# The high half of a weight against both halves of the tokens in one 512-column matmul

## The chip, the core and the metric

The program runs on one core of a Trainium2 chip. Its time is that of the device in microseconds for one launch; lower is better. A run of the kernel before is taken beside every run of another kernel on the same chip.

The engines of the core work side by side and meet only at semaphores. TensorE (PE in the rows) multiplies matrices, with a weight load (PEld) ahead of each matmul. VectorE (DVE), ScalarE (ACT) and GpSimd (POOL) do elementwise work, and SyncE (SP) starts most DMAs.

## The reference

Two blocks are computed on 256 tokens of width 1024, in float32. The first has two layers; each layer has a feed-forward stage, a mixer of four branches (two convolutions, two attentions), and a second feed-forward stage. The second block has an attention and a recurrent branch with a context of 256 more tokens and then a mixture of 32 experts. Only the four feed-forward stages of the first block matter here:

```python
D_MODEL = 1024; SEQ = 256; DEPTH = 2; D_FF = 2816

def _swiglu(x, w_gate, w_up, w_down):
    return (jax.nn.silu(x @ w_gate) * (x @ w_up)) @ w_down

for l in range(DEPTH):
    x = x + 0.5 * _swiglu(_rmsnorm(x, ffn1_norm[l]), ffn1_w_gate[l], ffn1_w_up[l], ffn1_w_down[l])
    ...
    x = x + 0.5 * _swiglu(_rmsnorm(x, ffn2_norm[l]), ffn2_w_gate[l], ffn2_w_up[l], ffn2_w_down[l])
```

## The kernel before

The program is a row of phases with a barrier between them. Activations are kept with features on the 128 partitions and the 256 tokens along the free dimension.

**Products in two halves.** TensorE multiplies here in the type fp32r, in which a number keeps fewer bits than float32. Each float32 operand is therefore split: `hi` is the number in fp32r, `lo` is what is left. A product is the sum of three: w_hi x_hi, w_hi x_lo and w_lo x_hi. The function `product` (L242) issues them as three matmuls of 256 columns, all accumulating in the same half bank of PSUM.

**A feed-forward stage** (`ffn_program`, L423) first normalizes x; VectorE and ScalarE write the halves `h_hi` and `h_lo` of the result, eight slices `k` of 128 features. Then it goes over 22 chunks `c` of 128 hidden features. For a chunk there are three weight tiles of 128 x 1024: `g` (gate), `u` (up) and `d` (down), each with two buffers `a`. The work on them is this:

- SyncE loads the tiles into `raw` (L442), three DMAs a chunk; a load waits until VectorE has made the `lo` half (`g_lo`, `u_lo`, `d_lo`) of the tile that was in the buffer.
- ScalarE casts each to `hi` (`upper`, L492), then computes silu of the gate part from PSUM into `sil` (L501).
- VectorE subtracts to make `lo` (`lower`, L515); then it multiplies `sil` by the up part in PSUM into `hid` (L523), and splits `hid` into two halves by a cast (L250) and a subtraction (L252).
- TensorE computes `gate_up(c)`: 2 x 8 products, 48 matmuls, into the PSUM bank 4 + a, the gate part in one half of it and the up part in the other. `down(c)` are 8 products, 24 matmuls, of the down tile with the halves of `hid`; they accumulate over all chunks in banks 0 to 3.

The order on each engine is as it is written. TensorE goes gate_up(c + 1), down(c), so that the hidden part of chunk c is made while gate_up(c + 1) runs. VectorE's turn for chunk c is: `lower` of gate and up of chunk c + 1, `lower` of down of chunk c, then wait for silu, `hid`, cast, subtraction. ScalarE's turn is: cast of gate and up of chunk c + 1, cast of down of chunk c, then silu of chunk c, for which it waits for TensorE alone (and for `hid` of two chunks before).

**GpSimd in these stages.** Beside this, in each of the four stages, GpSimd computes a quarter of a matrix-vector product that the second block needs (`ada_pool`, L377). It loads twelve tiles of `w_ada` with its own DMAs (L398), multiplies them by a row (L403, 16 such products, 128 x 1024) and adds each up by halving (L390: widths 512, 256, 128). It is done with that before the stage is.

Of the kernel before, what the change touches and what calls it, by code (L numbers as in the profile page):

```python
# [14 lines left out]
F32R = mybir.dt.float32r  # L15
I32 = mybir.dt.int32
ALU = mybir.AluOpType
ACT = mybir.ActivationFunctionType
# [344 lines left out]
def ffn_phase(nc, B, I, l, which, wg, wu, wd, gain):  # L363

    with ExitStack() as ctx:
        (raw, sil, hid) = alloc(nc, ctx, B, raw=(P, 6, D), sil=(P, 2, T), hid=(P, 2, T))
        (hi, lo, hid_hi, hid_lo) = alloc(nc, ctx, B, F32R, hi=(P, 6, D), lo=(P, 6, D), hid_hi=(P, 2, T), hid_lo=(P, 2, T))
        (B.c_rows, B.wada, B.adaprod, B.adasum) = alloc(
            nc, ctx, B, c_rows=(P, 2, D), wada=(P, 2, D), adaprod=(P, D), adasum=(P, 2 * ADA_CTX + ADA_X, D // 8))
        ffn_program(nc, B, l, dict(g=wg, u=wu, d=wd), gain, raw, hi, lo, sil, hid, hid_hi, hid_lo, (I["w_ada"], which))  # L370
# [52 lines left out]
def ffn_program(nc, B, l, src, gain, raw, hi, lo, sil, hid, hid_hi, hid_lo, ada):  # L423
    x, ps, con = B.x, B.ps, B.con
    acc = ps[:, 0:4, :].rearrange("p b (c t) -> p (b c) t", t=T)
    gu = [ps[:, 4 + a, :].rearrange("p (w t) -> p w t", t=T) for a in range(2)]
# [3 lines left out]
    with phase(nc, NORM + ADA + names + " gu_done silu_done hid_mul hid_hi_done hidden_ready down_done x_done") as (block, s):  # L430
# [16 lines left out]
        def _(pe):  # L447
# [5 lines left out]
            def gate_up(c, a):  # L453
                wait(pe, s["hidden_ready"], c - 1)
                for j, kind in enumerate("gu"):
                    pe.wait_ge(s[f"{kind}_lo"], c + 1)
                    for k in range(KD):
                        if kind == "g" and isinstance(c, int) and c == 0:
                            pe.wait_ge(s["h_lo_done"], k + 1)
                        w = slice(k * P, (k + 1) * P)  # L460
                        mm = product(nc, gu[a][:, j, :], hi[:, slot[kind] + a, w], lo[:, slot[kind] + a, w],
                                     B.h_hi[:, k, :], B.h_lo[:, k, :], k == 0, k == KD - 1)
# [22 lines left out]
        def _(act):  # L485
# [8 lines left out]
            def turn(c, a, end, i):  # L494
# [4 lines left out]
                act.wait_ge(s["gu_done"], c + 1)  # L499
                wait(act, s["hid_mul"], c - 1)  # L500
                nc.scalar.activation(sil[:, a, :], gu[a][:, 0, :], ACT.Silu).then_inc(s["silu_done"], 1)  # L501
# [9 lines left out]
        def _(dve):  # L511
# [5 lines left out]
            def turn(c, a, end, i):  # L517
# [3 lines left out]
                lower("d", c, a)  # L521
                dve.wait_ge(s["silu_done"], c + 1)
                nc.vector.tensor_tensor(hid[:, a, :], sil[:, a, :], gu[a][:, 1, :], ALU.mult).then_inc(s["hid_mul"], 1)  # L523
# [469 lines left out]
def first_block_program(nc, B, I):  # L993

    B.stage = "first"
    with ExitStack() as ctx:
        (B.vec, B.nsink, B.swa_table) = alloc(nc, ctx, B, vec=(P, NVEC), nsink=(P, 4), swa_table=(P, 4 * TC, T))
        B.h_hi, B.h_lo = alloc(nc, ctx, B, F32R, h_hi=(P, KD, T), h_lo=(P, KD, T))
# [1064 lines left out]
```

## Time and profile before

| | |
|---|---|
| runs | 3191.58, 3196.12, 3221.68 us; median 3196.12 |
| span of the profiled execution | 3212.8 us |
| its own time | not shown apart; it is at least the span |
| mean granted TensorE clock | 0.915 of full speed |
| TensorE busy, matmuls | 2749.1 us (86%), 17040 |
| VectorE busy | 1658.3 us (52%), 2343 instructions |
| ScalarE busy | 788.1 us (25%), 1190 instructions |
| GpSimd busy | 608.7 us (19%), 410 instructions |
| `lower` of the feed-forward stages (L515) | 264, 497.1 us busy, 1926 ns each |
| feed-forward stages, first to last silu | 63 to 243, 597 to 777, 830 to 1011, 1365 to 1544 us |

The stages can be told by the silu on L501, of which there are 22 in each. A matmul is pipelined: the time shown for one (some 0.28 us) is longer than the distance to the next, so TensorE's pace is read from the starts. A time that VectorE or GpSimd shows for one instruction runs from its start to its end and includes what it waited for in between.

### The profile page before, as it was taken

To read this page: it belongs to the slowest core of one execution; us is meant where nothing else is said; L and a number is where in the kernel's file an instruction comes from. 1 tells how busy PE (TensorE), PEld (TensorE's weight loads), DVE (VectorE), ACT (ScalarE), POOL (GpSimd) and SP (SyncE) were. 2 spreads that over 40 slices of the span, in tenths; PEclk is the share of its full clock that TensorE was granted. 3 is DMA by queue.
4 is the path that set the end of the run, shared out by engine and by line. 5 is a ranking of instruction groups with operands and counts; after the bars stand their busy time and mean duration, and the time that the engine had idled before them with its cause. 6 is when DMAs were issued, how large, how long until landed. Compare 5 with 4: busy or idle time off the path is not lost. (4 is left out here: it accounts for less than half of the span.)

```text
span 3212.8 us, 44631 instructions
## 1 busy us (share of the span) xinstructions
PE 2749.1 (86%) x17040; PEld 2031.2 (63%) x17040; DVE 1658.3 (52%) x2343; ACT 788.1 (25%) x1190; POOL 608.7 (19%) x410
## 2 busy tenths in 40 slices
PE   5998888898898898699598697568998999989986
PEld 4998777798798896699488565533433333333333
DVE  4974665994984376697413665342223233232323
ACT  2334441433343442234223321100000000000000
POOL 2940000770960000293000000001001101011010
PEclk9999879899899898899798798779789999999998
DMA  5653431563563351365114110539899999999993
GB/s 215 231 177 131 151 111 53 205 233 139 182 223 118 119 169 53 138 229 208 42 65 158 39 53 1 211 134 355 346 390 378 410 410 410 410 410 410 410 407 155
DMA packets 186745, 697.77 MB, mean 217 GB/s; under 512 B 20611, under 2 KB 22019, under 8 KB 185091
## 3 DMA queue, kind: packets, MB, share of 16 engines
q1 hardware_dynamic: 178742, 662.00, 54.6%
q0 software_dynamic: 7488, 29.36, 2.4%
q10 hardware_dynamic: 432, 5.33, 0.4%
q8 instruction: 48, 0.79, 0.1%
q14 instruction: 35, 0.29, 0.0%
HBM read 694.54 MB, written 2.11 MB: 217 GB/s over the span
## 5 line engine op out<-in xcount | busy, mean ns | idle before, releaser
L515 DVE TENSOR_TENSOR lo_first<-raw_first,hi_first 128x1024 fp32r<-128x1024 f32 x264 | 497.1, 1926 | 42.6 <-ACT hi_first L492 40.7
L1704 PE MATMUL ps<-wexp_all_second,hg_second 128*64 128x512 f32 x2112 | 475.5, 597 | 41.5 <-DMA wexp_all_second<-in_w_lin 24.3
L243 PE MATMUL ps<-h_hi_first,hi_first 128*128 128x256 f32 x1408 | 409.1, 291 | 48.9 <-DVE h_lo_first L234 48.8
L244 PE MATMUL ps<-h_lo_first,hi_first 128*128 128x256 f32 x1408 | 404.6, 287 | 0.0
L245 PE MATMUL ps<-h_hi_first,lo_first 128*128 128x256 f32 x1408 | 404.4, 287 | 0.0
L1704 PEld LDWEIGHTS ps<-wexp_all_second,hg_second 128*64 128x64 f32 x2112 | 149.4, 137 | 358.1 <-issue 283.9
L492 ACT CAST hi_first<-raw_first 128x1024 fp32r<-128x1024 f32 x264 | 267.8, 1048 | 206.0 <-DMA raw_first<-in_ffn_wg 132.0
L243 PEld LDWEIGHTS ps<-h_hi_first,hi_first 128*128 128x128 f32 x1408 | 275.7, 196 | 56.2 <-DVE h_lo_first L234 30.7
L243 PE MATMUL ps<-h_hi_first,w_hi_first 128*128 128x256 f32 x960 | 275.9, 287 | 34.7 <-DVE w_lo_first L338 23.8
L1792 DVE TENSOR_TENSOR sq_whole<-ps,con_all_whole 64x512 f32<-64x512 f32 x132 | 90.8, 688 | 402.8 <-POOL con_all_whole L1684 349.2
L244 PEld LDWEIGHTS ps<-h_lo_first,hi_first 128*128 128x128 f32 x1408 | 276.9, 197 | 0.0
L245 PEld LDWEIGHTS ps<-h_hi_first,lo_first 128*128 128x128 f32 x1408 | 276.7, 197 | 0.0
L244 PE MATMUL ps<-h_lo_first,w_hi_first 128*128 128x256 f32 x960 | 273.6, 285 | 0.0
L245 PE MATMUL ps<-h_hi_first,w_lo_first 128*128 128x256 f32 x960 | 273.3, 285 | 0.0
L1704 PE MATMUL ps<-wexp_all_second,aT_second 128*64 128x512 f32 x1056 | 244.0, 616 | 23.5 <-ACT aT_second L1771 23.5
L1792 DVE TENSOR_TENSOR y_second<-ps,con_all_whole 64x512 f32<-64x512 f32 x66 | 45.4, 688 | 324.7 <-PE ps L1704 324.2
L390 POOL TENSOR_TENSOR adaprod_first<-adaprod_first 128x512 f32<-128x512 f32 (+1 forms) x128 | 209.2, 1634 | 10.0
L243 PEld LDWEIGHTS ps<-h_hi_first,w_hi_first 128*128 128x128 f32 x960 | 186.3, 194 | 38.3 <-DVE w_lo_first L338 20.7
L338 DVE TENSOR_TENSOR w_lo_first<-raw_first,w_hi_first 128x1024 fp32r<-128x1024 f32 x120 | 146.8, 1225 | 117.5 <-ACT w_hi_first L313 106.6
L243 PE MATMUL ps<-hid_hi_first,hi_first 128*128 128x256 f32 x704 | 200.2, 284 | 4.8 <-DVE hid_lo_first L252 4.6
L244 PE MATMUL ps<-hid_lo_first,hi_first 128*128 128x256 f32 x704 | 199.2, 283 | 0.0
L245 PE MATMUL ps<-hid_hi_first,lo_first 128*128 128x256 f32 x704 | 199.2, 283 | 0.0
(354 smaller groups left out, 4635.8 us busy)
## 6 DMA issues: line engine op xcount, KB each, us to landing
wexp_all_second<-in_w_gate SPq DMA_DIRECT2D x66, 2048.0 KB, 17.7
wexp_all_second<-in_w_lin SPq DMA_DIRECT2D x66, 2048.0 KB, 24.6
wexp_all_second<-in_w_down SPq DMA_DIRECT2D x66, 2048.0 KB, 23.0
raw_first<-in_ffn_wg SPq DMA_DIRECT2D x88, 512.0 KB, 5.4
raw_first<-in_ffn_wu SPq DMA_DIRECT2D x88, 512.0 KB, 6.7
raw_first<-in_ffn_wd SPq DMA_DIRECT2D x88, 512.0 KB, 3.3
raw_first<-in_w_g SPq DMA_DIRECT2D x64, 512.0 KB, 3.3
wada_first<-in_w_ada POOLq DMA_DIRECT2D x48, 512.0 KB, 7.1
```

The costliest lines, as they stand in the source:

```text
L243: nc.tensor.matmul(out, w_hi, x_hi, start=start, stop=False, skip_group_check=True)
L244: nc.tensor.matmul(out, w_hi, x_lo, start=False, stop=False, skip_group_check=True)
L245: return nc.tensor.matmul(out, w_lo, x_hi, start=False, stop=stop, skip_group_check=True)
L338: nc.vector.tensor_tensor(B.w_lo[:, slot], B.raw[:, slot], B.w_hi[:, slot].bitcast(F32), ALU.subtract).then_inc(s[f"{tag}_lo"], 1)
L390: add = lambda out, x, width: nc.gpsimd.tensor_tensor(out, x[..., 0:width], x[..., width:2 * width], ALU.add)
L492: nc.scalar.copy(hi[:, slot[kind] + a % 2], raw[:, slot[kind] + a % 2]).then_inc(s[f"{kind}_hi"], 1)
L515: nc.vector.tensor_tensor(lo[:, j], raw[:, j], hi[:, j].bitcast(F32), ALU.subtract).then_inc(s[f"{kind}_lo"], 1)
L1704: mm = nc.tensor.matmul(dst[side(half), :], lhs(k), B.wexp[2 * "gld".index(kind) + part][:, k % 4, half * HALF:(half + 1) * HALF], start=( ...
L1792: last = tt(dst[side(half), :], bank[side(half), :], B.bias[side(half), n * D + half * HALF:n * D + (half + 1) * HALF], ALU.add)
```

## The change

`h_hi` and `h_lo` now lie side by side in one tile `h_pair`, 512 columns for each slice k. In `gate_up` the high half of a weight meets both in one matmul of 512 columns, which fills a whole PSUM bank: w_hi x_hi in columns 0 to 255, w_hi x_lo in columns 256 to 511. The third product, w_lo x_hi, is added to the first 256 columns. Gate and up so take a bank each, and a buffer `a` two banks (4 and 5, or 6 and 7; the mean square of the norm, in bank 6, is read before chunk 1 writes there). VectorE adds the two parts of gate and of up in one tensor_reduce that reads 1024 elements of PSUM in each partition and writes 512 to `sil` in SBUF. ScalarE takes silu of the gate part there, in place, once the reduce is done; VectorE's product `hid` then reads both operands from SBUF. `down` is as it was.

```diff
--- before.py
+++ after.py
@@ -363,7 +363,7 @@
 def ffn_phase(nc, B, I, l, which, wg, wu, wd, gain):
 
     with ExitStack() as ctx:
-        (raw, sil, hid) = alloc(nc, ctx, B, raw=(P, 6, D), sil=(P, 2, T), hid=(P, 2, T))
+        (raw, sil, hid) = alloc(nc, ctx, B, raw=(P, 6, D), sil=(P, 2, 2, T), hid=(P, 2, T))
         (hi, lo, hid_hi, hid_lo) = alloc(nc, ctx, B, F32R, hi=(P, 6, D), lo=(P, 6, D), hid_hi=(P, 2, T), hid_lo=(P, 2, T))
         (B.c_rows, B.wada, B.adaprod, B.adasum) = alloc(
             nc, ctx, B, c_rows=(P, 2, D), wada=(P, 2, D), adaprod=(P, D), adasum=(P, 2 * ADA_CTX + ADA_X, D // 8))
@@ -423,11 +423,11 @@
 def ffn_program(nc, B, l, src, gain, raw, hi, lo, sil, hid, hid_hi, hid_lo, ada):
     x, ps, con = B.x, B.ps, B.con
     acc = ps[:, 0:4, :].rearrange("p b (c t) -> p (b c) t", t=T)
-    gu = [ps[:, 4 + a, :].rearrange("p (w t) -> p w t", t=T) for a in range(2)]
+    gu = [ps[:, 4 + 2 * a:6 + 2 * a, :] for a in range(2)]
     ms = ps[:, 6, 0:T]
     slot = {"g": 0, "u": 2, "d": 4}
     names = " ".join(f"w{k}{a}" for k in "gud" for a in range(2)) + " " + " ".join(f"{k}_{h}" for k in "gud" for h in ("hi", "lo"))
-    with phase(nc, NORM + ADA + names + " gu_done silu_done hid_mul hid_hi_done hidden_ready down_done x_done") as (block, s):
+    with phase(nc, NORM + ADA + names + " gu_done added silu_done hid_mul hid_hi_done hidden_ready down_done x_done") as (block, s):
         s.update(std=B.std[:, 0:T], var=B.var[:, 0:T], rstd=B.rstd[:, 0:T])
 
         @block.gpsimd
@@ -458,8 +458,10 @@
                         if kind == "g" and isinstance(c, int) and c == 0:
                             pe.wait_ge(s["h_lo_done"], k + 1)
                         w = slice(k * P, (k + 1) * P)
-                        mm = product(nc, gu[a][:, j, :], hi[:, slot[kind] + a, w], lo[:, slot[kind] + a, w],
-                                     B.h_hi[:, k, :], B.h_lo[:, k, :], k == 0, k == KD - 1)
+                        nc.tensor.matmul(gu[a][:, j, :], hi[:, slot[kind] + a, w], B.h_pair[:, k, :], start=(k == 0),
+                                         stop=False, skip_group_check=True)
+                        mm = nc.tensor.matmul(gu[a][:, j, 0:T], lo[:, slot[kind] + a, w], B.h_hi[:, k, :], start=False,
+                                              stop=(k == KD - 1), skip_group_check=True)
                 mm.then_inc(s["gu_done"], 1)
 
             def down(c, a):
@@ -496,9 +498,8 @@
                     upper("g", c + 1, a + 1, i)
                     upper("u", c + 1, a + 1, i)
                 upper("d", c, a, i)
-                act.wait_ge(s["gu_done"], c + 1)
-                wait(act, s["hid_mul"], c - 1)
-                nc.scalar.activation(sil[:, a, :], gu[a][:, 0, :], ACT.Silu).then_inc(s["silu_done"], 1)
+                act.wait_ge(s["added"], c + 1)
+                nc.scalar.activation(sil[:, a, 0, :], sil[:, a, 0, :], ACT.Silu).then_inc(s["silu_done"], 1)
 
             def first():
                 upper("g", 0, 0, 0)
@@ -519,8 +520,11 @@
                     lower("g", c + 1, a + 1)
                     lower("u", c + 1, a + 1)
                 lower("d", c, a)
+                dve.wait_ge(s["gu_done"], c + 1)
+                nc.vector.tensor_reduce(sil[:, a], gu[a].rearrange("p w (h t) -> p w t h", h=2), AX,
+                                        ALU.add).then_inc(s["added"], 1)
                 dve.wait_ge(s["silu_done"], c + 1)
-                nc.vector.tensor_tensor(hid[:, a, :], sil[:, a, :], gu[a][:, 1, :], ALU.mult).then_inc(s["hid_mul"], 1)
+                nc.vector.tensor_tensor(hid[:, a, :], sil[:, a, 0, :], sil[:, a, 1, :], ALU.mult).then_inc(s["hid_mul"], 1)
                 dve.wait_ge(s["hid_mul"], c + 1)
                 wait(dve, s["down_done"], c - 1)
                 split_dve(dve, nc, hid[:, a, :], hid_hi[:, a, :], hid_lo[:, a, :], s["hid_hi_done"], s["hidden_ready"], c + 1)
@@ -995,7 +999,8 @@
     B.stage = "first"
     with ExitStack() as ctx:
         (B.vec, B.nsink, B.swa_table) = alloc(nc, ctx, B, vec=(P, NVEC), nsink=(P, 4), swa_table=(P, 4 * TC, T))
-        B.h_hi, B.h_lo = alloc(nc, ctx, B, F32R, h_hi=(P, KD, T), h_lo=(P, KD, T))
+        (B.h_pair,) = alloc(nc, ctx, B, F32R, h_pair=(P, KD, 2 * T))
+        B.h_hi, B.h_lo = B.h_pair[:, :, 0:T], B.h_pair[:, :, T:2 * T]
         with ExitStack() as small:
             (B.relb, B.line, B.c_row) = alloc(nc, small, B, relb=(N_BUCKETS, 4), line=(P, 4, 512), c_row=(1, 2 * D))
             swa_table_phase(nc, B, I)
```

On TensorE, at the start of the first feed-forward stage (`ps` is PSUM, `hi` and `lo` the halves of the weight, `h_...` those of the tokens), there stood before, for two slices k of the gate part:

```order
L243 MATMUL ps<-h_hi_first,hi_first 128x256
L244 MATMUL ps<-h_lo_first,hi_first 128x256
L245 MATMUL ps<-h_hi_first,lo_first 128x256
L243 MATMUL ps<-h_hi_first,hi_first 128x256
L244 MATMUL ps<-h_lo_first,hi_first 128x256
L245 MATMUL ps<-h_hi_first,lo_first 128x256
```

and now, for three slices:

```order
L461 MATMUL ps<-h_pair_first,hi_first 128x512
L463 MATMUL ps<-h_pair_first,lo_first 128x256
L461 MATMUL ps<-h_pair_first,hi_first 128x512
L463 MATMUL ps<-h_pair_first,lo_first 128x256
L461 MATMUL ps<-h_pair_first,hi_first 128x512
L463 MATMUL ps<-h_pair_first,lo_first 128x256
```

Two matmuls stand for three, with the same columns in all.

On VectorE, one turn in the loop over the chunks, before:

```order
L515 TENSOR_TENSOR lo_first<-raw_first,hi_first 128x1024 x2
L513 REGISTER_ALU
L515 TENSOR_TENSOR lo_first<-raw_first,hi_first 128x1024
L523 TENSOR_TENSOR hid_first<-sil_first,ps 128x256
L258 REGISTER_ALU
L250 CAST hid_hi_first<-hid_first 128x256
L252 TENSOR_TENSOR hid_lo_first<-hid_first,hid_hi_first 128x256
```

and now:

```order
L516 TENSOR_TENSOR lo_first<-raw_first,hi_first 128x1024 x2
L514 REGISTER_ALU
L516 TENSOR_TENSOR lo_first<-raw_first,hi_first 128x1024
L524 TENSOR_REDUCE sil_first<-ps 128x512
L527 TENSOR_TENSOR hid_first<-sil_first 128x256
L258 REGISTER_ALU
L250 CAST hid_hi_first<-hid_first 128x256
L252 TENSOR_TENSOR hid_lo_first<-hid_first,hid_hi_first 128x256
```

The reduce stands ahead of `hid`, which waits for a silu that itself waits for the reduce. On ScalarE the order is the same, but silu reads and writes `sil_first` where it read `ps`.

## Rows read from the trace of the kernel before

**Rows 1.** View by stretches: from:to, length, busy us (x instructions) per engine, clock, DMA
```profile
63.40:191.60 128.20, 126.91 (x1058) 126.71 (x1057) 126.43 (x89) 51.38 (x60) 116.73 (x77) 1.00 0.63 223
...
596.90:707.90 111.00, 110.23 (x915) 109.72 (x914) 109.58 (x79) 44.26 (x53) 100.34 (x68) 1.00 0.63 222
829.60:942.10 112.50, 110.11 (x914) 109.61 (x913) 109.90 (x80) 44.26 (x52) 98.50 (x63) 1.00 0.61 218
942.10:1011.00 68.90, 68.90 (x576) 68.90 (x576) 34.87 (x47) 25.01 (x30) 0.00 (x0) 1.00 0.42 147
1364.50:1474.90 110.40, 109.95 (x914) 109.51 (x913) 108.98 (x79) 44.10 (x52) 99.82 (x68) 1.00 0.63 223
```

**Rows 2.** Timeline of TensorE: start, us, instruction; two of six matmuls, 256 columns
```profile
200.06 0.28 PE L243 MATMUL ps<-hid_hi_first,hi_first 128*128 128x256 f32 x1
...
200.66 0.28 PE L245 MATMUL ps<-hid_hi_first,lo_first 128*128 128x256 f32 x1
```

**Rows 3.** Timeline of TensorE in the second block: two of six, 512 columns
```profile
1609.64 0.39 PE L244 MATMUL ps<-h_lo_second,w_hi_second 128*128 128x512 f32 x1
...
1610.77 0.39 PE L243 MATMUL ps<-h_hi_second,w_hi_second 128*128 128x512 f32 x1
```

**Rows 4.** Timeline of a quiet chunk: ScalarE's silu, then VectorE's turn
```profile
950.76 0.38 ACT L501 ACTIVATE sil_first<-ps 128x256 f32<-128x256 f32 x1 [4.71 <-PE ps L245]
...
951.17 0.42 DVE L523 TENSOR_TENSOR hid_first<-sil_first,ps 128x256 f32<-128x256 f32 x1 [3.85 <-ACT sil_first L501]
951.72 0.29 DVE L250 CAST hid_hi_first<-hid_first 128x256 fp32r<-128x256 f32 x1
952.04 0.43 DVE L252 TENSOR_TENSOR hid_lo_first<-hid_first,hid_hi_first 128x256 fp32r<-128x256 f32 x1
952.38 3.61 DVE L515 TENSOR_TENSOR lo_first<-raw_first,hi_first 128x1024 fp32r<-128x1024 f32 x3
```

**Rows 5.** Groups by line, all of the span: VectorE's reduces (xcount, busy, mean ns)
```profile
L1468 DVE TENSOR_REDUCE stat_second<-prob_second 128x1 f32<-128x512 f32 x16 | 11.0, 686 | 0.5
...
L1585 DVE TENSOR_REDUCE sel_second<-cmp_second 128x32 f32<-128x1024 f32 x2 | 2.4, 1220 | 0.1
```

**Rows 6.** Groups by line, VectorE in the stretch 63.4:191.6, GpSimd busy
```profile
L252 DVE TENSOR_TENSOR hid_lo_first<-hid_first,hid_hi_first 128x256 fp32r<-128x256 f32 x15 | 12.3, 819 | 0.5
L250 DVE CAST hid_hi_first<-hid_first 128x256 fp32r<-128x256 f32 x15 | 12.3, 819 | 1.1
L523 DVE TENSOR_TENSOR hid_first<-sil_first,ps 128x256 f32<-128x256 f32 x15 | 6.1, 407 | 0.0
```

**Rows 7.** The same in the stretch 596.9:707.9
```profile
L523 DVE TENSOR_TENSOR hid_first<-sil_first,ps 128x256 f32<-128x256 f32 x13 | 5.3, 408 | 0.0
```

**Rows 8.** Timelines of VectorE and GpSimd in one turn beside GpSimd
```profile
858.29 7.76 DVE L515 TENSOR_TENSOR lo_first<-raw_first,hi_first 128x1024 fp32r<-128x1024 f32 x3
...
858.02 0.59 POOL L398 DMA_DIRECT2D wada_first<-in_w_ada  x1 [0.65 <-POOL adasum_first L390]
858.64 2.41 POOL L403 TENSOR_TENSOR adaprod_first<-wada_first,c_rows_first 128x1024 f32<-128x1024 f32 x1
...
867.02 0.59 POOL L398 DMA_DIRECT2D wada_first<-in_w_ada  x1 [0.64 <-POOL adasum_first L390]
```

**Rows 9.** Timelines of ScalarE (two silus) and VectorE at a stage's start
```profile
596.97 0.39 ACT L501 ACTIVATE sil_first<-ps 128x256 f32<-128x256 f32 x1 [5.50 <-PE ps L245]
...
602.73 0.38 ACT L501 ACTIVATE sil_first<-ps 128x256 f32<-128x256 f32 x1 [2.55 <-PE ps L245]
...
600.10 7.41 DVE L515 TENSOR_TENSOR lo_first<-raw_first,hi_first 128x1024 fp32r<-128x1024 f32 x3
```

**Rows 10.** DMA issues: the slowest weights to land (xcount, KB, us)
```profile
raw_first<-in_ffn_wu SPq DMA_DIRECT2D x88, 512.0 KB, 6.7
```

**Rows 11.** View by stretches: a stretch of the mixer and one beside GpSimd
```profile
446.00:486.00 40.00, 33.67 (x93) 19.20 (x93) 21.81 (x76) 14.77 (x45) 0.00 (x0) 0.50 0.26 105
923.00:933.00 10.00, 8.49 (x70) 8.49 (x71) 9.91 (x7) 3.46 (x5) 9.53 (x7) 1.00 0.33 117
```

## The prediction

> **What bounds the kernel now.** I read the page's shares first (they stand in the table above): TensorE is by far the busiest, but a share over the whole span says nothing of one stage. The span holds four feed-forward stages (two in each of the two layers), and only they are changed. Next came the table by stretches. Each feed-forward stage has a first part in which GpSimd forms the products for `w_ada`, and a second part in which GpSimd is idle. In the four first parts, 462.1 us together, VectorE is busy for 454.9 us (126.43 + 109.58 + 109.90 + 108.98) and GpSimd for 415.4 us, so neither has room; TensorE is busy for 457.2 us. In a quiet part VectorE is busy for 34.87 of 68.90 us and TensorE for all of it [rows 1]. So TensorE sets the time everywhere in these stages, but in the first parts VectorE is level with it.
>
> TensorE's pace is the distance between starts, not the 0.28 us of one matmul: from 200.06 to 200.66 there are five steps of 0.120 us, 256 columns each [rows 2]. A chunk has 72 matmuls and takes 72 x 0.120 = 8.64 us. ScalarE's activations mark two ends of gate_up 5.76 us apart (596.97, 602.73), which is 48 x 0.120 [rows 9].
>
> **TensorE: the gain.** A chunk now issues, 16 times, a 512-column and a 256-column matmul where three of 256 stood; `down` keeps its 24. The columns stay the same, so only a cost per matmul can go. The trace has 512-column matmuls of the same type in the second block: from 1609.64 to 1610.77 five steps, 0.226 us each [rows 3]. Two of 256 cost 0.240, one of 512 costs 0.2265 (the middle of 0.226 and 0.227), so 0.0135 us goes each time: 0.216 us a chunk, which becomes 8.42 us; times 88 chunks, **-19 us**. This is an upper bound of the gain, since it needs TensorE to be what bounds. The lower bound is nothing. I take all of it for TensorE's own work and count its waits apart.
>
> The Trainium skill ("TensorE: Matmul & The Clock Gate", Back-to-back issue gap) gives a warm matmul N / 2.4 + 2.5 ns: one matmul fewer would save 2.5 ns, 3.5 us in all, and my sum would be 15 us higher. The trace disagrees: what lies above the column time is 13 ns here.
>
> **VectorE: the price.** A chunk on VectorE is three `lower` subtractions, the product `hid`, a cast and a subtraction. In a quiet chunk: 3.61 + 0.42 + 0.29 + 0.43 = 4.75 us, after a silu of 0.38 us on ScalarE [rows 4]. The change puts two things into that queue.
> - A tensor_reduce that reads 1024 elements of PSUM and writes 512. The trace has no such form. The nearest is a reduce of 1024 elements in SBUF to 32: 1.22 us [rows 5]. Below, it can't cost less than the trace's reduce of 512 elements, 0.69 us; above, if the strided reads go at half pace, the step of 0.53 us from 512 to 1024 elements is paid twice over on 1024: 2.3 us. I take 1.22, the row with its number of elements.
> - A wait for silu. So far silu ran as soon as TensorE was done, long before VectorE came to it. Now it starts after VectorE's own reduce, and VectorE stands: 0.38 plus two handovers. One of these is seen in the quiet chunk, 0.03 us (951.14 to 951.17) [rows 4]; with as much again, 0.45 us. What is queued behind this wait are the cast, the subtraction and the next chunk's three `lower`s, and TensorE waits for all of them.
>
> Together 1.67 us a chunk; bounds 1.1 and 2.8. `hid` keeps its 512 reads but both now come from SBUF; see below. ScalarE loses its lead as well: it casts the next gate half only after silu, 1.05 us later, while VectorE needs about 1.2 us to come to it. That costs nothing, cover 0.1 us. SyncE's loads wait for `d_lo`, come with VectorE's turn and still have more than a turn, 8.4 us, to land in 6.7 [rows 10]: nothing.
>
> Quiet parts: VectorE's turn becomes 4.75 + 1.67 = 6.4 us, against 8.42. It is hidden, with 2.0 us of cover. At the end of each stage the last `down` needs the last `hid`: 1.67 + 0.42 + 0.29 + 0.43 + 0.1 of gaps = 2.9 us, behind the 24 x 0.12 = 2.9 us of the `down` before. Nothing.
>
> **The parts with GpSimd.** Here 54 chunks pass (15 + 3 x 13, the count of the `hid` products [rows 6, 7]), 462.1 / 54 = 8.56 us each. VectorE's own work is 4.75 of that; the other 3.8 us is GpSimd. The two take turns at something that they share: between 858.29 and 866.05 three `lower`s last 7.76 us instead of 3.61, and GpSimd's operations lie in the gaps one by one, the 2.41 us product first [rows 8]. The cast and the subtraction are stretched as well (0.82 us each in the first stage's part, 0.29 and 0.43 when quiet), while `hid`, which reads PSUM, stays at 0.41 [rows 6]. So a reduce from PSUM should pass freely, and the new `hid`, which reads SBUF twice, should be stretched like the subtraction, by 0.82 - 0.43 = 0.4 us.
>
> How long is the new turn? If GpSimd takes 3.8 us from each turn as now: 4.75 + 1.67 + 3.8 = 10.2. With `hid` stretched too, 10.6. There is more: now the two have fallen into step, four operations of GpSimd to four gaps of VectorE. A pause of 1.67 us lets GpSimd start its 2.41 us product just before `hid`, and then each of `hid`, cast and subtraction meets one of its operations; counting one more meeting of 0.6 us gives 11.2. I take **10.7 us**, ends 10.2 and 11.2.
>
> How long are the parts? GpSimd's work is unchanged, so at most as now: 462 us. But it waits for VectorE too: of the 9.0 us from one load of `w_ada` (858.02) to the next (867.02) three `lower`s alone use 3.61 us by their quiet duration [rows 4, 8]. VectorE will leave the shared thing alone for 1.67 us more in each turn; if GpSimd gains most of that back, some 13%, the parts last 400 us. I take **440 us**, 41 turns.
>
> TensorE needs 41 x 8.42 = 345 us for them, so it stands still for 95. Some of it is a lead: at the start of a part VectorE is about 2.5 us ahead (the second `lower` of the three from 600.10 ends near 605.2, TensorE needs it at 602.73 + 2.88 + 2.88 = 608.5; `hid` is 2.4 us early) [rows 9]. Four leads take off 10. Today's own losses, 462.1 - 3801 matmuls x 0.120 = 6 us [rows 1], are in the time already and come off too. Left: **+79 us**.
>
> Sum: -19 + 79 = **+60 us**. Ends: 10.2 us and 400 us give 39.2 turns, 330 us of work, 70 - 16 - 19 = +35; 11.2 us and 462 us give 41.3 turns, 347 us, 115 - 16 - 19 = +80. The profiled execution's span is 3212.8 us; of the three runs shown only the slowest, 3221.68, is longer, so it is an execution about 20 us above the median. The sum on the median of 3196.12 is **3256 us**.
>
> **Rivals.**
> 1. *TensorE stays the bound* (not slower). Point of decision: in the parts with GpSimd the turn must stay under 8.42 us, so GpSimd's share must fall from 3.8 to 2.0 us a turn, because it does its work in the new pauses (1.67 us) instead of between the `lower`s. For it: GpSimd's total work is fixed, and an operation put into a pause blocks nobody. Against: VectorE is busy for 98% of these parts, and GpSimd for 90%; work that is put forward lets its next operation come sooner. If it holds in full: -19, 3177 us. If in part: between 3177 and 3228.
> 2. *The clock falls.* If TensorE idles 2.3 us in each turn of 10.7, it is busy for 79%. A stretch of 40 us in the mixer, TensorE busy for 84% of it, ran at a granted clock of 0.50, and 10 us of a feed-forward stage with 85% at 1.00 [rows 11]. At 1.2 GHz a chunk takes 16.8 us. If a third of the 440 us is at that level, 147 us do 73 us of TensorE's work instead of 0.79 x 147 = 116: +43, 3299 us.
> 3. *The reduce is dear*: 2.3 us instead of 1.22, or stopped by GpSimd as well. 1.1 x 41 = +45, which makes 3301 us; quiet turns would be 7.5 us and still hidden.
> 4. That the change doesn't do what it says I rule out: the order shows one 512- and one 256-column matmul for three, and the reduce ahead of `hid`.
>
> **How the numbers follow.** A measurement of this kernel tells about 1%, 32 us, from no change. My own case (+35 to +80) gets 0.53, the dear reduce 0.07, the clock 0.12: all slower. Rival 1 in full gets 0.10; a turn that grows by less than I count, -15 to +32 us, gets 0.15; 0.03 is for a gain above 1%, which the -19 us can't give. So faster 0.03, same 0.25, slower 0.72. The range 3192 to 3305 leaves out about 0.08 below, of rival 1, and 0.1 above, where rivals 2 and 3 are combined.
>
> **What would show it.** Step 1: starts 0.227 and 0.120 us apart in gate_up, 8.42 us a chunk in quiet parts. Step 2: reduce near 1.22 us with and without GpSimd, silu about 0.05 us behind it. Step 3: `hid` near 0.42 us when quiet, 0.8 beside GpSimd. Step 4: in the parts with GpSimd a turn of 10.2 to 11.2 us, and idle time of about 95 us on TensorE ahead of the first of `gate_up` or `down`, released by VectorE, where the four parts lose 6 us now. It would be wrong if GpSimd's parts got much shorter, if VectorE's operations there were stretched less than now, or if the granted clock left 1.00.

## The result, and the profile after

The changed kernel takes 3318.56 us (median of four runs, 3312.40 to 3346.33), the kernel before 3200.51 us (median of four). The ratio is 1.036, 95% interval 1.030 to 1.042: **slower by 3.6%**, some 118 us where +60 was forecast, above the end of the range. The way was right and the size was not. Some executions of these kernels show a lower granted clock and are some per cent longer; the ratios, and the medians of e1 and e2 below, leave them out, while the traces of e3 and e10 are of such executions.

The profiled execution took 3313.94 us, its span is 3312.3; before it was 3212.8. Most of those 99.5 us lie in the four feed-forward stages. As a measure of them I take, from the timelines, the time from the first `hid` of a stage to its last, summed over the four: 717.8 us before, **811.5 us** after, +93.7. (In the second stage before: 597.84 to 777.41; after: 630.77 to 832.49.) In all that follows "the stages" means this sum, which leaves out whatever varies in the second block.

The view by stretches, as in [rows 1]: the four parts in which GpSimd works, and the second stage's quiet part as the third row.

```profile
65.30:190.70 125.40, 104.95 (x620) 94.61 (x620) 117.92 (x77) 36.20 (x44) 112.63 (x82) 0.90 0.52 180
...
630.30:725.40 95.10, 76.42 (x451) 68.84 (x450) 90.42 (x56) 26.29 (x32) 85.74 (x61) 0.91 0.53 182
725.40:832.10 106.70, 106.70 (x703) 97.43 (x702) 73.05 (x89) 41.04 (x51) 1.50 (x5) 1.00 0.48 167
886.40:972.70 86.30, 67.39 (x399) 60.22 (x398) 81.41 (x49) 22.95 (x28) 77.76 (x56) 0.92 0.51 177
...
1445.90:1541.00 95.10, 76.78 (x451) 69.20 (x450) 90.35 (x56) 26.34 (x33) 85.68 (x61) 0.91 0.52 182
```

The parts are shorter, 401.9 us instead of 462.1, but only 34 chunks pass in them (11 + 8 + 7 + 8, counted as in [rows 6, 7]), 11.8 us each, where 54 passed before. VectorE is busy for 380.1 us of them and waits for silu in most of the rest. TensorE idles for 76 us and its granted clock is 0.90 to 0.92. In the quiet part TensorE is busy throughout, at 1.00. The waits say what it idled for, and what VectorE waits for in all 88 turns (engine, who waited, for whom: us, times, longest):

```profile
PE ps L243 <- DVE hid_lo_first L252: 76.4, 26, 4.9
...
DVE hid_first L527 <- ACT sil_first L502: 42.6, 88, 0.5
```

The groups of VectorE's operations in these stages over the whole span (count, busy, mean ns of one, idle before), first after, then before:

```profile
L516 DVE TENSOR_TENSOR lo_first<-raw_first,hi_first 128x1024 fp32r<-128x1024 f32 x264 | 428.7, 1675 | 33.3 <-ACT hi_first L494 32.3
...
L524 DVE TENSOR_REDUCE sil_first<-ps 128x512 f32<-128x1024 f32 x88 | 107.2, 1218 | 93.1 <-PE ps L463 92.8
...
L250 DVE CAST hid_hi_first<-hid_first 128x256 fp32r<-128x256 f32 x88 | 64.1, 729 | 8.8 <-DVE hid_first L527 4.8
...
L252 DVE TENSOR_TENSOR hid_lo_first<-hid_first,hid_hi_first 128x256 fp32r<-128x256 f32 x88 | 57.9, 658 | 3.0
L527 DVE TENSOR_TENSOR hid_first<-sil_first 128x256 f32<-128x256 f32 x88 | 55.3, 629 | 42.6 <-ACT sil_first L502 42.6
```

```profile
L515 DVE TENSOR_TENSOR lo_first<-raw_first,hi_first 128x1024 fp32r<-128x1024 f32 x264 | 497.1, 1926 | 42.6 <-ACT hi_first L492 40.7
...
L252 DVE TENSOR_TENSOR hid_lo_first<-hid_first,hid_hi_first 128x256 fp32r<-128x256 f32 x88 | 56.3, 640 | 3.0
...
L250 DVE CAST hid_hi_first<-hid_first 128x256 fp32r<-128x256 f32 x88 | 44.3, 503 | 6.2
...
L523 DVE TENSOR_TENSOR hid_first<-sil_first,ps 128x256 f32<-128x256 f32 x88 | 36.3, 412 | 109.8 <-ACT sil_first L501 109.8
```

The reduce costs 1.22 us and isn't stretched. `hid` is now stretched, 0.63 us in the mean instead of 0.41.

TensorE in a quiet part after:

```profile
770.08 0.28 PE L463 MATMUL ps<-h_pair_first,lo_first 128*128 128x256 f32 x1
770.20 0.40 PE L461 MATMUL ps<-h_pair_first,hi_first 128*128 128x512 f32 x1
770.43 0.28 PE L463 MATMUL ps<-h_pair_first,lo_first 128*128 128x256 f32 x1
770.54 0.40 PE L461 MATMUL ps<-h_pair_first,hi_first 128*128 128x512 f32 x1
770.78 0.28 PE L463 MATMUL ps<-h_pair_first,lo_first 128*128 128x256 f32 x1
```

A pair, 512 and 256 columns, takes 0.35 us. Over the 128 pairs from 746.8 to 815 the 256-column matmul starts 236 ns behind the 512-column one, and the next follows 117 ns later: 353 ns, against 3 x 120 = 360 before and the 346.5 that I took from [rows 2, 3]. The chunk takes 8.53 us, not 8.42.

One long turn beside GpSimd, VectorE and then GpSimd:

```profile
689.87 0.43 DVE L527 TENSOR_TENSOR hid_first<-sil_first 128x256 f32<-128x256 f32 x1 [0.48 <-ACT sil_first L502]
690.33 2.84 DVE L250 CAST hid_hi_first<-hid_first 128x256 fp32r<-128x256 f32 x1
693.21 1.43 DVE L252 TENSOR_TENSOR hid_lo_first<-hid_first,hid_hi_first 128x256 fp32r<-128x256 f32 x1
694.56 6.81 DVE L516 TENSOR_TENSOR lo_first<-raw_first,hi_first 128x1024 fp32r<-128x1024 f32 x3
701.29 1.21 DVE L524 TENSOR_REDUCE sil_first<-ps 128x512 f32<-128x1024 f32 x1
702.99 0.62 DVE L527 TENSOR_TENSOR hid_first<-sil_first 128x256 f32<-128x256 f32 x1 [0.48 <-ACT sil_first L502]
...
690.65 2.36 POOL L403 TENSOR_TENSOR adaprod_first<-wada_first,c_rows_first 128x1024 f32<-128x1024 f32 x1
693.09 2.13 POOL L390 TENSOR_TENSOR adaprod_first<-adaprod_first 128x512 f32<-128x512 f32 x2
695.30 1.32 POOL L390 TENSOR_TENSOR adasum_first<-adaprod_first 128x128 f32<-128x128 f32 x1
...
697.88 2.40 POOL L403 TENSOR_TENSOR adaprod_first<-wada_first,c_rows_first 128x1024 f32<-128x1024 f32 x1
700.36 2.97 POOL L390 TENSOR_TENSOR adaprod_first<-adaprod_first 128x512 f32<-128x512 f32 x2
```

It lasts 13.1 us from one `hid` to the next. `hid` itself just slips in. The cast waits for the whole product (690.65 to 693.01), the subtraction and each `lower` for one of GpSimd's adds or for the next product. In this one turn GpSimd gets through nearly two products, where before it was one in a turn of 9.0 us [rows 8].

### The profile page after: what moved, and what is told of

Its sections match the earlier page's. It is cut to its first block and busy times, and to the rows that moved or that the text cites. A ratio compares the mean times of both kernels' runs of the same rounds, so it can differ in the third digit from the quotient of the medians.

```text
span 3312.3 us, 41823 instructions
## 1 busy us (share of the span) xinstructions
PE 2767.1 (84%) x15632; PEld 1974.2 (60%) x15632; DVE 1740.0 (53%) x2431; ACT 780.5 (24%) x1190; POOL 566.0 (17%) x410
## 5 line engine op out<-in xcount | busy, mean ns | idle before, releaser
L461 PE MATMUL ps<-h_pair_first,hi_first 128*128 128x512 f32 x1408 | 519.3, 410 | 50.2 <-DVE h_pair_first L234 50.2
L516 DVE TENSOR_TENSOR lo_first<-raw_first,hi_first 128x1024 fp32r<-128x1024 f32 x264 | 428.7, 1675 | 33.3 <-ACT hi_first L494 32.3
L463 PE MATMUL ps<-h_pair_first,lo_first 128*128 128x256 f32 x1408 | 401.6, 285 | 0.0
L461 PEld LDWEIGHTS ps<-h_pair_first,hi_first 128*128 128x128 f32 x1408 | 272.0, 193 | 124.1 <-DVE h_pair_first L234 32.8
L243 PE MATMUL ps<-h_pair_first,w_hi_first 128*128 128x256 f32 x960 | 276.5, 288 | 36.7 <-DVE w_lo_first L338 25.0
L463 PEld LDWEIGHTS ps<-h_pair_first,lo_first 128*128 128x128 f32 x1408 | 274.2, 195 | 0.0
L244 PE MATMUL ps<-h_pair_first,w_hi_first 128*128 128x256 f32 x960 | 274.2, 286 | 0.0
L245 PE MATMUL ps<-h_pair_first,w_lo_first 128*128 128x256 f32 x960 | 274.1, 286 | 0.0
L243 PEld LDWEIGHTS ps<-h_pair_first,w_hi_first 128*128 128x128 f32 x960 | 187.6, 195 | 40.0 <-DVE w_lo_first L338 21.9
L243 PEld LDWEIGHTS ps<-hid_hi_first,hi_first 128*128 128x128 f32 x704 | 146.6, 208 | 88.9 <-DVE hid_lo_first L252 86.3
L244 PEld LDWEIGHTS ps<-h_pair_first,w_hi_first 128*128 128x128 f32 x960 | 188.3, 196 | 0.0
L245 PEld LDWEIGHTS ps<-h_pair_first,w_lo_first 128*128 128x128 f32 x960 | 186.4, 194 | 0.0
```

The source lines that it names most:

```text
L243: nc.tensor.matmul(out, w_hi, x_hi, start=start, stop=False, skip_group_check=True)
L244: nc.tensor.matmul(out, w_hi, x_lo, start=False, stop=False, skip_group_check=True)
L245: return nc.tensor.matmul(out, w_lo, x_hi, start=False, stop=stop, skip_group_check=True)
L461: nc.tensor.matmul(gu[a][:, j, :], hi[:, slot[kind] + a, w], B.h_pair[:, k, :], start=(k == 0), stop=False, skip_group_check=True)
L463: mm = nc.tensor.matmul(gu[a][:, j, 0:T], lo[:, slot[kind] + a, w], B.h_hi[:, k, :], start=False, stop=(k == KD - 1), skip_group_check=True)
L516: nc.vector.tensor_tensor(lo[:, j], raw[:, j], hi[:, j].bitcast(F32), ALU.subtract).then_inc(s[f"{kind}_lo"], 1)
```

## The experiments

Theories at the start. **A**: VectorE sets the turn beside GpSimd, since the two take turns at something shared; without GpSimd the change is harmless. **B**: VectorE's new work is too long anyway. **C**: the fall of the granted clock makes the difference between forecast and result. **D** and **E**: the extra time in TensorE's pair of matmuls comes from the second one adding into columns that are still being written (D), or from the order of the two shapes (E). **F**: the late silu and the stretched `hid` cost most, not the reduce. **G**, set against a later form of A in e10 to e12: GpSimd takes a share of each turn, paced or not. Ratios are to the kernel before on the same chip.

| | ratio (95%) | stages us | turn beside GpSimd us |
|---|---|---|---|
| before | 1 | 717.8 | 8.8 |
| changed | 1.036 (1.030, 1.042) | 811.5 | 11.9 |
| e1 before, GpSimd apart | 1.121 (no interval) | 714.2 | |
| e2 changed, GpSimd apart | 1.116 (1.109, 1.123) | 703.9 | |
| e3 changed, filler of 8 | 1.061 (1.053, 1.068) | 929.7 | 13.0 |
| e4 changed, other half | 1.028 (1.021, 1.034) | 807.8 | 11.9 |
| e5 before + reduce | 1.015 (1.005, 1.025) | 777.5 | 10.4 |
| e6 before, late silu | 1.003 (0.999, 1.007) | 726.0 | 9.1 |
| e7 before, `hid` from SBUF | 1.005 (1.001, 1.010) | 738.7 | 9.2 |
| e8 changed, reduce early | 1.014 (1.010, 1.018) | 761.4 | 9.8 |
| e9 changed, filler of 4 | 1.038 (1.032, 1.045) | 826.6 | 11.9 |
| e10 before, paced | 0.999 (0.995, 1.002) | 714.5 | 8.6 |
| e11 changed, paced | 1.005 (1.001, 1.009) | 726.9 | 8.9 |
| e12 changed, early, paced | 1.004 (1.001, 1.007) | 723.8 | 8.8 |

The turn is the mean over the time in which GpSimd works, from `hid` to `hid`, mean of the four stages; in e1 and e2 GpSimd works behind the stages.

**e1 and e2: GpSimd out of the way.**

```diff
         ffn_program(...)
+        with phase(nc, ADA) as (block, s):
+            @block.gpsimd
+            def _(pool):
+                ada_pool(pool, nc, s, B, l, I["w_ada"], which)
...
-        @block.gpsimd
-        def _(pool):
-            ada_pool(pool, nc, s, B, l, *ada)
```

e1. 

> The kernel before, with GpSimd's work for w_ada taken out of the four feed-forward stages and done in a phase of its own behind each. Same results. Theory A (VectorE and GpSimd take turns at something shared, and that alone brings VectorE level with TensorE): each stage runs at 8.64 us a chunk throughout, so it loses the 6 us of waits, and gains four phases of some 100 us: about +390 us on the kernel before (350 to 440). Rival B (VectorE's own work is too long, with or without GpSimd) expects the same of this kernel; it is the reference for the next.

e2. 

> The changed kernel with GpSimd's work apart in the same way. Theory A: without GpSimd the added 1.67 us a turn is hidden, each chunk takes 8.53 us, and this kernel is 10 us FASTER than e1 (5 to 20). Rival B (the reduce and the wait for silu cost by themselves, 1.67 us x 88 turns at most): it is slower than e1 by up to 147 us, and by at least 30.

The median of e1 is 3599.21 us (of two executions, +389 on the kernel before), that of e2 3581.93 (of four), 17 us less, as A expected. The stages take 714.2 and 703.9 us: without GpSimd the changed form is 10.3 us faster. B, which expected e2 to be slower by 30 us or more, falls. The two `lower` and `hid` groups of e2 show nothing stretched:

```profile
L516 DVE TENSOR_TENSOR lo_first<-raw_first,hi_first 128x1024 fp32r<-128x1024 f32 x264 | 307.9, 1219 | 34.8 <-ACT hi_first L494 33.9
...
L527 DVE TENSOR_TENSOR hid_first<-sil_first 128x256 f32<-128x256 f32 x88 | 37.4, 425 | 42.6 <-ACT sil_first L502 42.6
```

So the change is worth -10 us on TensorE, and everything else that it costs comes from the parts beside GpSimd: 93.7 + 10.3 = 104 us. The other 7 of the 17 us lie outside the stages. e2 takes GpSimd's loads of `w_ada` out of the stages as well; that its operations cost the time and not its loads is read from the timelines, as in the long turn above, where VectorE's cast ends just behind GpSimd's product.

**e5, e6 and e7: one of the three prices at a time, on the kernel before.**

```diff
 # e5 (the tile spare is allocated in lines left out here)
                 dve.wait_ge(s["silu_done"], c + 1)
+                nc.vector.tensor_reduce(B.spare, gu[a].unsqueeze(3).broadcast_to([P, 2, T, 2]), AX, ALU.add)
 # e6
                 wait(act, s["hid_mul"], c - 1)
+                act.wait_ge(s["d_lo"], c + 1)
 # e7 (sil is twice as large, as in the changed kernel)
-                nc.scalar.activation(sil[:, a, :], gu[a][:, 0, :], ACT.Silu)
+                nc.scalar.copy(sil[:, a, 1, :], gu[a][:, 1, :])
+                nc.scalar.activation(sil[:, a, 0, :], gu[a][:, 0, :], ACT.Silu)
...
-                nc.vector.tensor_tensor(hid[:, a, :], sil[:, a, :], gu[a][:, 1, :], ALU.mult)
+                nc.vector.tensor_tensor(hid[:, a, :], sil[:, a, 0, :], sil[:, a, 1, :], ALU.mult)
```

e5. 

> The kernel before with one tensor_reduce more in each of VectorE's turns, ahead of hid: it reads 1024 elements of PSUM and writes 512 to a spare tile, and nothing waits for it. So it is the reduce's time alone, without the late silu and without hid reading SBUF. Theory A: a turn beside GpSimd grows from 8.56 us by about 1.2 to 9.8, GpSimd ends a bit earlier, some 44 turns: +45 us on the kernel before (30 to 65). Rival F (the wait for silu and the stretched hid are what costs, not VectorE's own time): under +15 us.

e6. 

> The kernel before, but ScalarE's silu waits for VectorE's lower of the down tile, the operation ahead of hid, so that VectorE stands for silu in each turn beside GpSimd as it does in the changed kernel. No instruction is added. Theory A: 0.45 us a turn, 8.56 to 9.0, +15 us (5 to 25). Rival F: most of the change's cost, +60 us or more.

e7. 

> The kernel before, but ScalarE also copies the up part from PSUM into SBUF, so that VectorE's hid reads both operands from SBUF, as in the changed kernel. Theory A: hid is stretched beside GpSimd from 0.41 to 0.8 us or more; +0.4 us a turn: +12 us (0 to 25). Rival F: +40 us or more. If hid isn't stretched and the time stays, the stretching isn't a matter of where the operands lie.

In the stages e5 costs 59.7 us (its turn is 10.4 us where 9.8 was expected), e6 8.2, e7 20.9; together 88.8 of the 104. By their ratios e5 (+48 us, 15 to 81) and e7 (+17 us, 3 to 31) are clear of no change, and e6 isn't. The reduce is the main cost, and F falls, though `hid` from SBUF is dearer than the late silu. The prices hold for the place where each stands: e8, next, takes off 50 us by the order alone. That `hid` is stretched for its operands' place is shown by e7's group, 0.88 us in the mean where it was 0.41; so these two engines don't meet at semaphores alone. The Trainium skill ("GPSIMD Engine Reference", Specifications) says that GpSimd's way to SBUF is shared with VectorE, and that VectorE's operations with two SBUF inputs or in a two-port mode contend for it; this pair of kernels agrees:

```profile
L524 DVE TENSOR_TENSOR hid_first<-sil_first 128x256 f32<-128x256 f32 x88 | 77.0, 875 | 134.9 <-ACT sil_first L502 134.8
```

**e8: the same work in another order.**

```diff
-                lower("d", c, a)
                 dve.wait_ge(s["gu_done"], c + 1)
                 nc.vector.tensor_reduce(sil[:, a], ...).then_inc(s["added"], 1)
+                lower("d", c, a)
```

> The changed kernel with VectorE's reduce moved ahead of the lower of the down tile, so that silu runs while that lower does, and VectorE doesn't stand for it. Same work. Theory A: 0.45 us less in each of some 34 turns beside GpSimd: 15 us faster than the changed kernel (5 to 25), so about +100 on the kernel before. Rival F: 40 us faster or more.

It is 50 us faster in the stages, not 15: more than the removed wait can give, and my expectation missed it. A turn of VectorE and the start of the next, then GpSimd:

```profile
642.70 1.21 DVE L523 TENSOR_REDUCE sil_first<-ps 128x512 f32<-128x1024 f32 x1
643.83 1.21 DVE L516 TENSOR_TENSOR lo_first<-raw_first,hi_first 128x1024 fp32r<-128x1024 f32 x1
644.96 0.95 DVE L527 TENSOR_TENSOR hid_first<-sil_first 128x256 f32<-128x256 f32 x1
645.95 0.44 DVE L250 CAST hid_hi_first<-hid_first 128x256 fp32r<-128x256 f32 x1
646.43 0.43 DVE L252 TENSOR_TENSOR hid_lo_first<-hid_first,hid_hi_first 128x256 fp32r<-128x256 f32 x1
646.82 4.56 DVE L516 TENSOR_TENSOR lo_first<-raw_first,hi_first 128x1024 fp32r<-128x1024 f32 x2
651.30 1.21 DVE L523 TENSOR_REDUCE sil_first<-ps 128x512 f32<-128x1024 f32 x1
...
641.77 3.86 POOL L390 TENSOR_TENSOR adaprod_first<-adaprod_first 128x512 f32<-128x512 f32 x2
...
647.50 2.80 POOL L403 TENSOR_TENSOR adaprod_first<-wada_first,c_rows_first 128x1024 f32<-128x1024 f32 x1
```

The turn has settled at 8.6 us (642.70 to 651.30). GpSimd's adds now run under the reduce, which doesn't mind, and the `lower` behind it starts unhindered, 1.21 us; the engines are in step again, one product to a turn. In the changed kernel reduce and silu stood side by side, and GpSimd used the pause to start a whole product just ahead of three short operations. F's "40 us or more" would fit the number, but e6 says what the wait by itself costs, 8 us. That the start of a product in the pause makes the other 42 us is read from these turns; no run here varies it alone.

**e3 and e9: does the clock matter?**

```diff
-            with pe.Fori(1, FC // 2) as i:
+            def filler():
+                for b in range(8):    # e9: range(4)
+                    nc.tensor.matmul(ps[:, b % 4, :], con("zeros")[:, 0:P], con("zeros"), start=False, stop=False, ...)
...
+            with pe.Fori(1, 5) as i:
+                gate_up(2 * i, 0)
+                filler()
+                down(2 * i - 1, 1)
...
+            with pe.Fori(5, FC // 2) as i:
```

e3. 

> The changed kernel, with eight 512-column matmuls with a weight of zeros ahead of down of chunks 1 to 8 of each stage (1.8 us each time at full clock), which add zeros to the sums, so that TensorE idles less beside GpSimd. Theory A (VectorE alone sets the turn there, and the granted clock of 0.91 only fills TensorE's idle time): within 8 us of the changed kernel, about +118 on the kernel before, with the granted clock near 1.00. Rival C (the fall of the clock is what makes the change cost more than forecast): 20 to 36 us faster than the changed kernel (0.09 of 402 us).

e9. 

> As e3 with four matmuls instead of eight. In e3 one of them took 429 ns, so eight filled 3.4 us of a turn in which TensorE idled for 2.2 us; it became the bound itself. Four take 1.7 us. Theory A: TensorE's idle time in the stages (76 us) falls to some 25 us, the granted clock beside GpSimd rises from 0.91 to 0.95 or more, and the sum of the four stages from the first to the last hid stays within 8 us of the changed kernel's 811.5 us. Rival C (the clock): that sum falls by 15 us or more.

e3 was mis-sized: its filler has operands in float32 and not in fp32r, and such a matmul of 512 columns takes 429 ns from start to start, not 226, so TensorE became the bound (stages 929.7 us). e9 is the test. Two of its four parts with GpSimd:

```profile
63.10:187.80 124.70, 121.34 (x679) 97.04 (x678) 117.25 (x77) 36.21 (x44) 112.84 (x82) 1.00 0.52 181
627.60:724.70 97.10, 94.97 (x519) 74.72 (x518) 91.80 (x60) 28.15 (x35) 87.36 (x65) 1.00 0.52 185
```

The granted clock is 1.00 where it was 0.90 and 0.91, and TensorE idles for only 12.9 us in the stages. In the first two stages VectorE's turns are the same as in the changed kernel nearly one by one (second stage: 12.8, 9.9, 13.4, 13.2, 9.9, 13.2, 9.8, 13.1 against 12.8, 9.9, 13.4, 13.1, 9.9, 13.1, 9.9, 13.0 us), in the other two they come in part in another order, with the same mean of 11.9 us over all. So the clock doesn't set the turn, and C falls. The stages take 15 us more than the changed kernel's, which A didn't expect either: the filler leaves TensorE behind when GpSimd stops, and the turns just after that last 9.7 to 12.0 us in three of the stages instead of 6.4 to 7.7.

**e4: TensorE's pair.**

```diff
-                        mm = nc.tensor.matmul(gu[a][:, j, 0:T], lo[...], B.h_hi[:, k, :], ...)
+                        mm = nc.tensor.matmul(gu[a][:, j, T:2 * T], lo[...], B.h_hi[:, k, :], ...)
```

> The changed kernel, but the third product, low half of the weight, is added into columns 256 to 511 of the bank instead of columns 0 to 255; the reduce adds both, so the result is the same. Theory D (the 256-column matmul starts 236 ns behind the 512-column one, not 226, because it accumulates into columns that are still being written): the pair takes 346 ns instead of 353, quiet chunks 8.42 us instead of 8.53, and the kernel is 6 us faster than the changed one (3 to 10). Rival E (the order of the shapes costs that, wherever it writes): the pair stays at 353 ns, no change.

```profile
769.98 0.40 PE L461 MATMUL ps<-h_pair_first,hi_first 128*128 128x512 f32 x1
770.22 0.28 PE L463 MATMUL ps<-h_pair_first,lo_first 128*128 128x256 f32 x1
770.33 0.40 PE L461 MATMUL ps<-h_pair_first,hi_first 128*128 128x512 f32 x1
```

The pair stays at 236 + 117 ns (means of 128), so D falls. The stages are 3.7 us shorter, but the quiet chunk is the same 8.53 us; the ratio's interval overlaps that of the changed kernel. That the order of shapes causes it is not shown, only that the target columns don't.

**e10 to e12: GpSimd's products spread over the stage.** After e5 to e8 I added up how much VectorE's operations are stretched over the whole span: (mean - quiet duration) x count, with 1.22, 0.42, 0.29 and 0.43 us for `lower`, `hid`, cast and subtraction. Before: 264 x 0.706 + 88 x 0.214 + 88 x 0.210 = 224 us. Changed: 264 x 0.455 + 88 x 0.209 + 88 x 0.439 + 88 x 0.228 = 197 us. e5, by the same sum from these groups, also 197 us, e8 184. The groups of e5:

```profile
L516 DVE TENSOR_TENSOR lo_first<-raw_first,hi_first 128x1024 fp32r<-128x1024 f32 x264 | 446.5, 1742 | 35.4 <-ACT hi_first L493 34.6
...
L524 DVE TENSOR_REDUCE spare_first<-ps 128x512 f32<-128x1024 f32 x88 | 107.2, 1218 | 109.8 <-ACT sil_first L502 109.8
...
L252 DVE TENSOR_TENSOR hid_lo_first<-hid_first,hid_hi_first 128x256 fp32r<-128x256 f32 x88 | 65.2, 740 | 3.0
...
L250 DVE CAST hid_hi_first<-hid_first 128x256 fp32r<-128x256 f32 x88 | 57.1, 649 | 8.8 <-DVE hid_first L525 4.8
...
L525 DVE TENSOR_TENSOR hid_first<-sil_first,ps 128x256 f32<-128x256 f32 x88 | 35.9, 408 | 0.0
```

That is 2.9 to 3.5 us for each of the 64 products (GpSimd's last adds are counted in), with turns of 8.8 to 11.9 us. This gave theory **A'**: GpSimd takes a fixed time for its fixed work. Then it should be enough to deal it out evenly:

```diff
             if v:
                 pool.wait_ge(s["a_op"], n)
+            if products >= 4:
+                pool.wait_ge(s["gu_done"], 1 + (products - 4) * 8 // 5)
```

e10. 

> The kernel before, with GpSimd's products from the fifth on held back by a wait for TensorE's gate_up, so that one product falls on 1.6 chunks instead of one on each. Theory A': GpSimd takes some 3.7 us from VectorE with each product, whatever the length of VectorE's turn. A turn then is 4.75 + 3.7 / 1.6 = 7.1 us on the average, under 8.64: no waits, stages 714 us (717.8 before), 4 us faster on the whole. Rival G (GpSimd takes a share of each turn, paced or not): no difference in the stages beyond 1 us.

e11. 

> The changed kernel with GpSimd paced in the same way. Theory A': a turn is 6.42 + 3.7 / 1.6 = 8.7 us against 8.53, nearly level: the stages take 704 to 725 us instead of 811.5, some 90 to 105 us faster than the changed kernel, and so within 10 us of the kernel before. Rival G: a turn stays near 12 us where GpSimd works, and it works for longer: 800 us or more.

e12. 

> The changed kernel with the reduce ahead of the lower of the down tile (as e8) and GpSimd paced. Theory A': a turn is 5.97 + 3.7 / 1.6 = 8.3 us, under 8.53: the stages take 704 us as in e2 (up to 712), and the kernel is 6 to 14 us FASTER than the kernel before, the first that beats it. Rival G: as e8 or slower, 761 us.

```profile
613.50:771.60 158.10, 155.04 (x1017) 141.19 (x1016) 137.54 (x130) 61.15 (x75) 79.17 (x67) 1.00 0.62 212
...
L518 DVE TENSOR_TENSOR lo_first<-raw_first,hi_first 128x1024 fp32r<-128x1024 f32 x264 | 363.8, 1428 | 33.8 <-ACT hi_first L496 33.1
...
L529 DVE TENSOR_TENSOR hid_first<-sil_first 128x256 f32<-128x256 f32 x88 | 68.7, 781 | 42.6 <-ACT sil_first L504 42.6
L250 DVE CAST hid_hi_first<-hid_first 128x256 fp32r<-128x256 f32 x88 | 67.3, 764 | 8.7 <-DVE hid_first L529 2.4 <-PE ps L245 2.3
L252 DVE TENSOR_TENSOR hid_lo_first<-hid_first,hid_hi_first 128x256 fp32r<-128x256 f32 x88 | 61.6, 700 | 3.0
```

(First a stretch of e11's second stage, then its groups.) With a wait in GpSimd's queue alone the changed kernel's stages fall from 811.5 to 726.9 us, and the whole from +3.6% to +0.5%. That is 1.9 us above the end of what I expected of e11 (704 to 725). e10 takes 714.5 us where 714 were expected. In the middle of a stage e11's turns are 8.4 to 8.7 us; what is left lies in the first turns, before the pacing sets in (up to 12.8 us), and in GpSimd's last adds (one turn of 11.8 us in each stage). G, which expected 800 us or more, falls. e12 takes 723.8 us and not the 704 to 712 that I expected, for the same reason: the first stage, in which GpSimd starts late and does four products at once, has five turns of 10 to 12 us.

The sum of the stretching, by the same formula, doesn't quite bear A' out: 201 us in e10, but 175 in e12 and, from the groups above, 152 in e11, 2.4 us for each product. The new wait does two things at once: it spreads the products, and it lets each start as soon as gate_up is done, which is also when VectorE begins its reduce. In e11's second stage a reduce starts at 748.00 and a product at 748.12, so most of the product's 2.40 us lie under the reduce and the wait for silu. e10 has no reduce to hide a product under, and its waits still go; but there were only 6 us of waits to win. How much of the 85 us comes from the spreading and how much from this place in the turn, no run here separates.

No version here beats the kernel before by anything that can be told: the most that is to be had is 717.8 - 703.9 = 14 us, 0.4%.

## Why the prediction was wrong in size

- **What bounds, and where**: right. VectorE beside GpSimd was level with TensorE, quiet parts stayed with TensorE (e2).
- **TensorE's gain, -19 us**: half of it. -10.3 us (e1, e2); the pair takes 353 ns and not 346.5. I joined two durations, each taken from a row of equals, and their mixture costs 6.5 ns more.
- **VectorE's own price, 1.67 us a turn**: right. The reduce takes 1.22 us (1.21 to 1.23), silu with both handovers 0.48 where I had 0.45. That costs nothing in quiet parts: right.
- **"If GpSimd takes 3.8 us from each turn as now"**: this is the step that failed. I had 3.8 us a turn for GpSimd, 4.3 in the 10.7 that I took and 4.8 at the upper end; measured are 11.8 - 6.42 = 5.4 us. GpSimd doesn't take the same from each turn, it takes a time that goes with its own work, 197 us in all after and 224 before, for its 64 products. When the turn grows, fewer turns share that. I took the length of the parts (440 us) and the length of the turn (10.7 us) as two free numbers, but they hang together: turns = (length - GpSimd's time) / VectorE's own turn. With the measured values, (401.9 - 197) / 6.42 = 32; counted are 34, so the formula holds to some 6%. My own length of 440 us would have given (440 - 197) / 6.42 = 38 turns instead of 41, or 34 with the 224 us of before. The length was off too, by 38 us, and the other way: with 401.9 us and my 10.7 us a turn the sum would have been +50, so the number came nearer than the step deserved.
- **The sum**: measured, 401.9 - 34 x 8.53 = 112 us, less my 10 for the lead and 6 lost before, is +96 where I had +79; with -10 for TensorE +86. The stages say +93.7, and the remaining 8 us I can't assign (the 10 for the lead are my forecast, no run shows them): e4, with the same mean turn, has +90. Outside the stages the two profiled executions differ by another 6 us; the 118 us between medians of four holds the spread of the runs too (12 us is 0.4%).
- **Ends**: the turn of 11.8 us lies above my upper end of 11.2. The mechanism that I gave for that end, a pause that lets GpSimd start a product ahead of `hid`, is what the long turn shows, but it hits cast, subtraction and the first `lower` too. e8 puts a size to it: the same work in an order without that pause costs 50 us less.
- **Rival 2, the clock**: it did fall, to 0.90 to 0.92, which I had named as a sign of being wrong, but e9 shows that it only fills time in which TensorE would have waited. So TensorE's idle time is 76 us and not some 95, though more is lost. **Rival 1** lacked its condition: GpSimd did get done earlier, but not by working in pauses that cost VectorE nothing. **Rival 3**: the reduce was not dear and was not stretched.

## What to carry to other kernels

Where two engines take turns at something shared, the one takes from the other a time that goes with its own work more than with the other's loop: length = turns x own work + that time. It isn't a constant: here it was 184 to 228 us (e8, e7) where GpSimd ran freely and VectorE set the pace, and 152 where most products started with the reduce (e11). Work that is added to a saturated engine then costs more than its duration, since fewer turns get done beside the same disturbance, and its place in the order counts as much as its length. Before a loop is changed that runs beside such an engine, see whether the disturber can be paced, or started where it does no harm; here one wait in its queue did both and took back 85 of 94 us.

## What the hardware showed that I had not expected

- A 512-column matmul followed by one of 256 columns: 236 and 117 ns from start to start (sum 353), where rows of equals take 226.5 and 120 (346.5). The columns written don't matter (e4).
- Of VectorE's operations beside GpSimd, the reduce from PSUM stayed at 1.22 us and `hid` at 0.41 with one operand in PSUM; with both in SBUF it had 0.88 in the mean (e7). The single-operand cast from SBUF is stretched too, from 0.29 to 1.0 us in the mean in e10.
- A float32 matmul of 512 columns takes 429 ns at a granted clock of 1.00 (e3), against the 226.5 of [rows 3] in fp32r.
